# The order tables of a two-layer hybrid mixer, rewritten for four engines

## The reference

```
xn = rms_norm(h, g_mix);  proj = xn @ w_in
c_q, a_k, a_v, i_k, i_w, m_q, m_k, m_v, m_o, m_i, m_f = split(proj)
c_q = rms_norm(c_q);  a_q = c_q @ w_q_up;  i_q = c_q @ w_iq_up
a_q, a_k = rope(rms_norm(a_q)), rope(rms_norm(a_k));  i_q = rope(i_q);  i_k = rope(rms_norm(i_k))
for each block of 128 queries:          # att
    score = sum over 8 heads of w_idx * relu(i_q . i_k), causal
    sel   = top 128 keys of score;  o = softmax(a_q . a_k[sel] / 8) @ a_v[sel]
m_q, m_k = silu(causal_conv(m_q, m_k))  # mLSTM, 4 heads of 128
d[t,s] = exp(b[t] - b[s] + i[s] - m[t]) for s <= t
hm  = ((m_q . m_k) * d) @ m_v / max(|sum of the same|, exp(-m[t]))
h   = h + concat(att, sigmoid(m_o) * rms_norm(hm)) @ w_out
```

## Time and profile before

| | us |
|---|---|
| three runs | 2075.06, 2075.58, 2077.3 |
| the profiled execution, in all | 2075.06 |
| span of its trace | 2073.2 |
| mixer of layer 0 in it, from `ikf` to the last `wo` | 712.2 to 937.2 |
| mixer of layer 1 in it | 1398.6 to 1624.3 |
| mean granted clock of PE | 0.997 |

### The profile page before, as it was taken

The page is one execution under the profiler, slowest core; times in us unless marked ns, Lnnn a source line. Parts: engine busy times, 40 slices in busy tenths (PEclk is TensorE's granted clock), DMA queues, the critical chain, the costliest instruction groups (busy, mean ns, idle before and its releaser), DMA issues.

```text
span 2073.2 us, 26448 instructions
## 1 busy us (share of the span) xinstructions
PE 2027.9 (98%) x10252; PEld 1583.7 (76%) x10252; DVE 1122.5 (54%) x1997; ACT 867.1 (42%) x1381; POOL 919.5 (44%) x1160
## 2 busy tenths in 40 slices
...
DMA packets 188300, 194.28 MB, mean 94 GB/s; under 512 B 8592, under 2 KB 184080, under 8 KB 187792
## 3 DMA queue, kind: packets, MB, share of 16 engines
...
q10 hardware_dynamic: 576, 3.15, 0.4%
...
HBM read 190.48 MB, written 2.10 MB: 93 GB/s over the span
## 4 chain that ended last, share of the span: by engine, by line
PE 89%; DVE 5%; POOL 2%; ACT 2%; DMA 1%; issue 1%; SPq 0%; DVEq 0%; ACTq 0%; POOLq 0%
PE ps L803 20%; PE ps L805 20%; PE ps L804 20%; PE ps L822 3%; PE ps L824 3%; PE ps L823 3%; POOL wl L2837 2%; PE ps L850 2%; PE ps L839 1%; PE ps L840 1%; PE ps L841 1%; DVE mix L2457 1%; PE ps L1349 1%; PE ps L1422 1%; PE ps L1405 1%; PE ps L907 1%
## 5 line engine op out<-in xcount | busy, mean ns | idle before, releaser
L2837 POOL TENSOR_TENSOR wl<-ring,wh 128x256 fp32r<-128x256 f32 x1008 | 752.8, 780 | 821.9 <-ACT wh L1459 821.9
L1459 ACT ACTIVATE wh<-ring 128x1024 fp32r<-128x1024 f32 (+1 forms) x298 | 308.9, 1044 | 310.0 <-PE ps L805 256.6
L803 PE MATMUL ps<-xh,wh 128*128 128x512 f32 (+1 forms) x976 | 383.4, 393 | 2.3 <-POOL wl L2837 2.3
L805 PE MATMUL ps<-xh,wl 128*128 128x512 f32 (+1 forms) x976 | 380.4, 390 | 0.0
L804 PE MATMUL ps<-xl,wh 128*128 128x512 f32 (+1 forms) x976 | 380.4, 390 | 0.0
L803 PE MATMUL ps<-acts,wh 128*128 128x512 f32 x880 | 344.1, 391 | 0.7 <-POOL wl L2837 0.4
L805 PE MATMUL ps<-acts,wl 128*128 128x512 f32 x880 | 342.4, 389 | 0.0
L804 PE MATMUL ps<-acts,wh 128*128 128x512 f32 x880 | 342.4, 389 | 0.0
L2457 DVE SCALAR_TENSOR_TENSOR mix<-ps,par,mix 128x441 f32<-128x441 f32 (+2 forms) x352 | 213.7, 686 | 30.9 <-ACT mix L1690 30.9
L803 PEld LDWEIGHTS ps<-xh,wh 128*128 128x128 f32 (+1 forms) x976 | 183.0, 188 | 46.7 <-issue 8.8
L805 PEld LDWEIGHTS ps<-xh,wl 128*128 128x128 f32 (+1 forms) x976 | 182.9, 187 | 39.3
...
## 6 DMA issues: line engine op xcount, KB each, us to landing
...
early<-in_w_ada_dram SPq DMA_DIRECT2D x7, 1024.0 KB, 10.8
```

What stands on the lines that cost most here:

```text
L803: t.matmul(b[0:m, 0:n], s.hi[:, k, a:a + m], x2[0][:, k, :], start=k == ks[0], stop=False)
L805: i = t.matmul(b[0:m, 0:n], s.lo[:, k, a:a + m], x2[0][:, k, :], start=False, stop=k == ks[-1])
L1459: a.activation(s.hi[:, :, c], s.ap[:, :, c], ACT.Copy).then_inc(*up("hi", "hi", name, hf))
L2837: i = p.tensor_tensor(s.lo[:, k:k + 2, c], s.ap[:, k:k + 2, c], s.hi[:, k:k + 2, c].bitcast(F32), ALU.subtract)
```

## The change

The four strings of `LAYER` are written in another order. The entries are the same, each with its count, and so are all shapes; beyond them nothing in the file is touched. The largest moves:

- PE: `mqk.1.0` and `cqT` change places around the `tok`, `mqk.1.0` is now ahead of the `up` steps and `ikT` stands among them; in layer 1 `ikf` is ahead of `fold`. In the middle, `mv.1.2`, `mv.1.3` and `qk.3.*` change places; the `S` steps stand in another order. At the end, `wo.1` and `er.1` come ahead of `er.0`, `wo.2`, `wo.0`.
- ACT: `iksq`, `gE`, `toko.1.1`, `ikroot`, `gL` ahead of all `upo`; `gexp` of heads 0 and 1 in one run; `ho.2` ahead of `den`.
- DVE: `sd`, `rsum` and `top` steps in another order. POOL: `gap`, `mask` and the low halves in another order.

```
-        tok0@1246 fold@3 ikf@0 tok.1.0@5 ikfT@7 cqT.1@6 cqT.0@0 tok.1.1@3 up.0.1@0 up.1.0@1 up.0.3@7 up.0.0@6
+        tok0@1246 ikf@0 fold@3 tok.1.0@5 ikfT@7 tok.1.1@3 cqT.0@0 cqT.1@6 mqk.1.0@5 up.0.3@7 up.1.0@1 ikT@2 up.1.1@4
...
-        toko.1.1 gE upo.0.1 upo.0.3 toko.1.0 gL upo.1.0 ikroot hi.mqk.0.0 upo.0.0 upo.0.2 upo.1.1 upo.1.3 upo.1.2 qsq
...
+        toko.0.1 iksq gE toko.1.1 ikroot gL upo.0.3 upo.1.0 upo.1.1 upo.1.3 upo.0.1 upo.0.0 upo.0.2 upo.1.2 qsq ikTo
...
-        gap.0.3 gap.1.2 gap.0.0 gap.0.2 gap.0.1 gap.1.3 gap.1.1 gap.1.0 lo.mqk.3.1 mask.1.2 mask.1.1 lo.mqk.3.0
+        gap.0.2 gap.1.2 gap.0.1 gap.1.1 gap.1.0 gap.1.3 gap.0.0 gap.0.3 mask.1.3 mask.0.0 mask.1.1 lo.mqk.3.1
```

More of the change, by code:

```diff
@@ L259 @@
-        pt.2.3@63 mo.2.1 mo.3.1 pt.2.2@46 qk.1.0@37 S.2.1@1 qk.1.1@46 S.3.0@5 pv.2.2 pv.2.3 S.2.0@7 S.2.3@6 S.3.1@4
-        S.2.2@3 pt.1.0@51 qk.1.2@37 pt.1.1@46 pv.1.0@5 S.3.3@0 num.1.0@37 qk.1.3@01 num.1.1 pt.1.2@46 pv.1.1 num.1.2
-        pt.1.3@10 num.1.3 pv.1.2 pv.1.3 nn@4 denT@6 nnT@1 wo.2@4 wo.0@7 er.0@26 er.1@53 wo.1@0 wo.3@1""",
-    "scalar": """
-        hi.tok.2.0 cs.0 cs.3 root hi.tok.1.0 hi.tok.1.1 cs.2 cs.1 cqroot ikfo toko.0.1 toko.0.0 hi.mqk.0.1 iksq
-        toko.1.1 gE upo.0.1 upo.0.3 toko.1.0 gL upo.1.0 ikroot hi.mqk.0.0 upo.0.0 upo.0.2 upo.1.1 upo.1.3 upo.1.2 qsq
[L265 to L277, removed]
@@ L278 @@
-    "vector": """
[L279 to L292, removed]
@@ new lines @@
+        up.1.3@3 up.0.1@0 up.0.0@6 up.0.2@7 up.1.2@1 tok.1.2@4 iT.0@3 iT.1@0 tok.1.3@6 ix.3.1@71 iT.2@2 ix.3.0@43
+        ix.2.0@06 iT.3@2 mqk.1.1 ix.3.2@24 qT.2@3 qT.0@7 qT.1@3 qT.3@1 mqk.4.0@7 ix.3.3@31 kT.1@2 mqk.0.0@4 ix.2.3@32
+        ix.2.1@10 kT.0@6 mqk.0.1 ix.2.2@16 mqk.5.0@0 ix.1.0@16 mqk.5.1 ix.1.3@32 rsT@1 mqk.4.1 ix.1.1@61 mv.0.0@5
+        mqk.3.0@4 ix.1.2@16 qk.0.0@50 mqk.3.1 qk.0.1@16 mqk.2.0@7 gT@05 mqk.2.1 pt.0.0@16 mv.0.1@3 pt.0.1@16 pv.0.0@2
+        qk.0.3@05 aT@3 qk.0.2@16 pv.0.1 M.0@05 thT@1 mv.1.0@6 mv.1.1@3 pt.0.3@10 qk.3.1@57 mv.1.2@4 pt.0.2@10
```

46 lines of the change are left out of this document (42 added, 4 removed).

## The result

The changed kernel is slower: 2087.56 us (median of 4 runs, 2085.72 to 2090.27) against 2075.32; ratio 1.0063, 95% interval 1.005 to 1.0077 (a ratio here need not be the quotient of the two medians). The forecast was 2080.3 with a range of 2071 to 2085: the sign is right, the size is not, 12.2 us instead of 4.7 to 5.2. The 16 later runs of it lay between 2085.4 and 2093.2, with a median of 2089.5, so its time is known to about 2 us.

A forecast was written before the change was run, and what follows sets the result against it. PE was taken to bound the kernel, busy 2027.9 of 2073.2 us. Layer 0 +1.7 and layer 1 +2.05 gave +3.75 on 2075.06, 2078.8; one clock drop, +1.5, made 2080.3, range 2071 to 2085.

The forecast's parts named there:

- What is late next is the queries' chain: Front: `qsq` ends near 744.0 instead of 741.3; PE waits 1.9 us in all at `qT.2`, `qT.0` and two others.
- Front of layer 0: -1.3: Layer 0's front: 1.9 us of waits where it had 3.2, so 1.3 us saved.
- the front of layer 1: Layer 1's front: 0.65 at `ikf` plus 1.9 at the queries, less 3.7 for the old stop and clock: -1.15 us.
- costed at nothing: Behind the middle stop: reordered softmax and mLSTM steps have more cover, so 0; each that fails costs some tenths.
- loses most: End of the mixer: `nn` loses most of its 0.6 us wait, since `hsq.2` and `hsq.3` are adjacent.
- I count one drop of two, +1.5: Clock: of the two new stops, one in each layer, one brings a fall to half rate, +1.5 us.
- The sum: Both mixers: layer 0 +1.7, layer 1 +2.05, together +3.75 us, then +1.5 for the clock: 2080.3.
- the stop in the middle: PE ahead of `qk.3.0` in both layers, waiting for `pto.0.2` behind seven `gexp`: 2.9 us, 3.3 with gaps at 11.25.
- mild gain: Rival, the middle does not stop: front's gains stay, 2073.0; 18% with its faster case, 0.06 for the mild gain.
- cancelling case: Rival: the middle stop is near 1.5 us, so gains and losses cancel at 2076; 22%.
- `ikn` was short: Front: `ikn` needs 2.6 to 3.7 us, ending before 730; the rival had it stay at 6 us, 2083.6, 15%.
- the same mechanism one step on: Case of the clock dropping twice, at the middle stop of both layers: 2081.8, counted in the forecast's range.

The follow-up runs named there:

- a_kn: Changed kernel with one move on DVE, `kn` back behind `score.3.3` instead of behind `score.3.1`: 2088.1 us, ratio 1.0057.
- a_all: Changed kernel with three moves: `pto.0.2` three `gexp` earlier on ACT, `kn` back behind `score.3.3`, `nnc` ahead of the `u2h` copies: 2085.6 us, ratio 1.0044.
- a_nnc: Changed kernel with the end of ACT's order altered, `nnc` ahead of the `u2h` copies and `ho.2` behind them: 2088.7 us, ratio 1.0059.

## Why the prediction was wrong

**The front: right in its steps, one missing.** `ikroot` runs at 725.56 (forecast 726), without POOL beside it `ikn` is done at 728.2, and a 128x32 operation takes 0.18 us where it took 0.77:

```profile
725.89 0.18 DVE L2636 RECIPROCAL arena_m<-arena_m 128x4 f32<-128x4 f32 x1 [0.35 <-ACT arena_m L1846]
...
727.23 0.18 DVE L2573 TENSOR_TENSOR arena_m<-arena_m,rope 128x32 f32<-128x32 f32 x1
...
727.88 0.29 DVE L2643 COPY arena_m<-arena_m 128x256 f32<-128x256 f32 x1
```

`iT.0` starts at 744.11 without a wait (forecast 744.3), `ikf` of layer 1 waits 0.64 (0.65), `qT.2` 0.49 (0.45), `qT.0` 0.90 and 1.46 (1.15), and nothing falls near 1432. What the forecast did not have is `kT.1`: 1.63 us, with 0.20 behind it, in layer 0 and 1.07 and 0.20 in layer 1. DVE's rows, then ACT's, then PE's:

```profile
760.53 0.64 DVE L2571 TENSOR_TENSOR arena_m<-arena_m,rope 128x64 f32<-128x64 f32 x1
...
761.79 0.77 DVE L2573 TENSOR_TENSOR arena_m<-arena_m,rope 128x64 f32<-128x64 f32 x1
...
763.66 2.46 DVE L2682 SCALAR_TENSOR_TENSOR arena_m<-arena_m 128x512 f32<-128x512 f32 x3
```

```profile
764.45 0.60 ACT L1464 ACTIVATE arena_m<-ps 128x512 f32<-128x512 f32 x1 [4.13 <-DVE arena_m L2682]
```

```profile
765.10 0.66 PE L850 MATMUL ps<-con,arena_m 128*128 128x128 f32 x4 [1.63 <-ACT arena_m L1464]
```

`kn` had been moved two `score` steps ahead. It takes 5.4 us here (3.2 before), its first three operations of 128x64 at 0.64 to 0.77 us while POOL makes low halves, and the next at 0.21. `relu.3.4` waits until `score.3.2` behind it has freed a buffer, and the bank of `kT.1` hangs on `relu.3.4`. That chain is in the rows, but `kn`'s place is the smaller part of the cause: with `kn` moved back 1.0 us stays, released by `kn` itself (a_kn, a_all). Why `kn` is late for `kT.1` is not settled. The step of the prediction that fails here is "What is late next is the queries' chain": it looked no further than `qrope`. So "Front of layer 0: -1.3" became 0, 3.2 us of waits before and 3.2 now, and the front of layer 1 waits 4.0 us where 2.55 were forecast.

**The middle: right place, low size.** The stop is where it was forecast, released by ACT's line 1464, 3.26 us for 2.9. POOL's gaps, then ACT's and PE's rows:

```profile
812.18 11.35 POOL L2905 TENSOR_SCALAR arena_m<-arena_m 128x256 f32<-128x256 f32 x8 [3.41 <-ACT arena_m L1464]
```

```profile
822.87 1.52 ACT L1956 ACTIVATE arena_m<-arena_m 128x512 f32<-128x512 f32 x3 [1.66 <-POOL arena_m L2905]
824.29 0.43 ACT L1464 ACTIVATE arena_m<-ps 128x128 f32<-128x128 f32 x2
```

```profile
824.86 1.13 PE L1349 MATMUL ps<-arena_m,mix 64*128 64x512 f32 x4 [3.26 <-ACT arena_m L1464]
```

PE reached `qk.3.0` 12.0 us after the start of `M.0` (forecast 11.9). The eight gaps took 11.35 us in a row, and the forecast had taken 10.8, for an overlap that its rows don't show: in the earlier trace rows the seven gaps start 1.57 us of idle time after the first one ends. 11.25 was its upper value, with 3.3 us for the stop, and that was the better one. The steps between this stop and `nn`, costed at nothing, have no wait of 0.1 us or more in the changed trace.

**The end.** `nn` 0.02 (forecast "loses most"), `nnT` 1.88 (2.0). Not seen: the order of `u2`, by which `wo.1` waits for the last of four copies, 0.2 us in layer 0 and 0.6 in layer 1. It is small only because the wait at `nnT` covers it; a_nnc uncovered 2.5.

**The clock: the term that was mis-sized.** "I count one drop of two, +1.5": there were four, two in each layer, and the forecast had left out that the stop at `nnT`, also in both layers, could bring one as well. The sum had one new fall in and the one near 1432 out, 1.5 less 1.5 us. The profile has four in and one out, three more, and beyond the idle time the two layers show 2.8 and 2.1 us for them: 4.9 us where the sum had nothing.

**What the distance is made of.** The idle time of the two mixers grew by 8.4 us, where the terms of the sum had 5.3. Of these 3.1 us, 2.8 are in the front. With the 4.9 us of the clock that is 8.0, about the distance of 7.8 us between 2080.3 and the 2088.1 of the profiled execution. The two steps that failed are the count of the clock's falls and the front's waits; the stop in the middle, which gave the sign, was forecast by its mechanism.

**The rivals.** Neither the mild gain nor the cancelling case came true, and `ikn` was short. That the clock falls twice, called "the same mechanism one step on", was still too mild.
